# Expert stage of a hybrid trunk step: U and V rows in two rings of eight, gathers in turns, routing cut into pieces

## What is computed

```python
qh = _f32(xt @ w_q).reshape(PEER_TBLOCK, PEER_HEADS, 2, PEER_HALF)
s = jnp.einsum('thpd,hpnd->thpn', qh, _f32(subkeys))
v_top, i_top = lax.top_k(s, PEER_TOPK)
cand = (v_top[:, :, 0, :, None] + v_top[:, :, 1, None, :]).reshape(...)
sc, pos = lax.top_k(cand, PEER_TOPK)
eidx = jnp.take_along_axis(cidx, pos, axis=-1).reshape(PEER_TBLOCK, PEER_HEADS * PEER_TOPK)
gate = jax.nn.softmax(sc, axis=-1).reshape(PEER_TBLOCK, PEER_HEADS * PEER_TOPK)
act = jax.nn.gelu(_f32(jnp.einsum('td,ted->te', xt, u_tab[eidx])))
return jnp.einsum('te,ted->td', (gate * act).astype(xt.dtype), v_tab[eidx])
```

## Time and profile before

| | us |
|---|---|
| median of 3 timed runs | 5029.88 |
| lowest and highest | 5022.36 and 5049.08 |
| profiled execution, its span (first to last instruction) | 5223.8 |
| of it PE, DVE, ACT, POOL busy | 3691.8, 2919.2, 712.4, 2823.9 |
| expert stage of layer 0 in the profiled execution | 653.7 to 2680.4 |
| expert stage of layer 1 | 3225.8 to 5223.8 |

### The profile page before, as it was taken

The page is one execution under the profiler, slowest core; times in us unless marked ns, Lnnn a source line. Parts: engine busy times, 40 slices in busy tenths (PEclk is TensorE's granted clock), DMA queues, the critical chain, the costliest instruction groups (busy, mean ns, idle before and its releaser), DMA issues. The chain is left out here.

```text
span 5223.8 us, 46315 instructions
## 1 busy us (share of the span) xinstructions
PE 3691.8 (71%) x13478; PEld 1958.6 (37%) x13478; DVE 2919.2 (56%) x7010; ACT 712.4 (14%) x2058; POOL 2823.9 (54%) x2687
## 2 busy tenths in 40 slices
PE   5987857767667757667569767677667667767765
PEld 3456433333333333333224454333333333333332
DVE  1025566556566656666640356666566666666676
ACT  0011011010111101111110331111111110111111
POOL 0000067666677676777620101777777777777765
PEclk7988978878888878888789778888888888888877
DMA  7100779889999998999851002999999999999997
GB/s 269 64 9 14 257 286 368 319 330 339 346 355 357 350 360 305 349 365 350 327 196 48 21 22 100 356 352 354 340 350 348 358 342 358 354 352 344 357 351 285
DMA packets 456668, 1476.66 MB, mean 283 GB/s; under 512 B 48180, under 2 KB 93940, under 8 KB 456212
## 3 DMA queue, kind: packets, MB, share of 16 engines
q0 software_dynamic: 368640, 1342.34, 69.5%
q1 hardware_dynamic: 87828, 131.85, 7.5%
HBM read 1469.20 MB, written 4.82 MB: 282 GB/s over the span
## 5 line engine op out<-in xcount | busy, mean ns | idle before, releaser
L1400 PE MATMUL ps<-big,y 128*128 128x512 f32 x2544 | 1288.2, 670 | 971.9 <-issue 495.1
L1579 DVE SCALAR_TENSOR_TENSOR big<-big,wrk 128x1024 f32<-128x1024 f32 x960 | 1175.3, 1226 | 688.5 <-DMA big<-in_peer_u,qk 609.7
L1493 POOL DMA_INDIRECT big<-in_peer_u,qk x960 | 1071.2, 1116 | 446.1 <-issue 276.8
L1400 PEld LDWEIGHTS ps<-big,y 128*128 128x128 f32 x2544 | 544.2, 218 | 1669.2 <-issue 1329.8
L1493 POOL DMA_INDIRECT big<-in_peer_v,qk x960 | 1001.2, 1043 | 292.7 <-issue 292.7
L1400 PE MATMUL ps<-big,diag 128*128 128x512 f32 x1248 | 548.3, 592 | 0.0
L1400 PE MATMUL ps<-mod,diag 128*128 128x512 f32 x1248 | 548.3, 592 | 0.0
L1579 DVE SCALAR_TENSOR_TENSOR mod<-mod,wrk 128x1024 f32<-128x1024 f32 x320 | 391.8, 1226 | 120.0 <-DMA mod<-in_peer_u,qk 113.1
L1493 POOL DMA_INDIRECT mod<-in_peer_u,qk x320 | 378.9, 1184 | 125.0 <-issue 91.9
L293 PE MATMUL ps<-wrk 128*128 128x512 f32 x960 | 415.1, 594 | 0.0
L1493 POOL DMA_INDIRECT mod<-in_peer_v,qk x320 | 302.8, 946 | 97.7 <-issue 95.8
(11 more groups left out here) (322 smaller groups left out, 3478.2 us busy)
## 6 DMA issues: line engine op xcount, KB each, us to landing
wrk<-in_ada_w SPq DMA_DIRECT2D x12, 2048.0 KB, 8.8
big<-in_ada_w SPq DMA_DIRECT2D x24, 1024.0 KB
big<-in_peer_u,qk POOLq DMA_INDIRECT x960
big<-in_peer_v,qk POOLq DMA_INDIRECT x960
mod<-modulation_rows SPq DMA_DIRECT2D x24, 512.0 KB, 6.6
wrk<-in_mlstm_w_in SPq DMA_DIRECT2D x6, 2048.0 KB, 8.0
wrk<-in_gla_w_in SPq DMA_DIRECT2D x6, 2048.0 KB, 8.1
lnw<-in_peer_w_q SPq DMA_DIRECT2D x8, 1024.0 KB
```

What stands on the lines that cost most here:

```text
L1400: mm = pe.matmul(m.ps[:, v_bank(b) + h, :], diag[r], ring[r][:, h * HALF:(h + 1) * HALF], start=r == 0, stop=r == rows - 1)
L1493: pool.indirect_dma_start(ring[r], None, table, bass.IndirectOffsetOnAxis(ap=stage[b][:, r:r + 1], axis=0))\
L1579: dve.scalar_tensor_tensor(out=ring[r], in0=ring[r], scalar=1.0, in1=xm[t], op0=ALU.mult, op1=ALU.mult, accum_out=act_u[b][:, r:r + 1]).th ...
```

## The change

The single ring of 16 becomes two rings of eight, one for U and one for V. POOL issues V row r of group G and U row r of group G+1 in turns, each with a wait of its own for the buffer's last use eight rows before, and reads the indices where the routing writes them. DVE's routing of group G+2 is cut into 14 pieces: the first stands in gelu, the others one behind each of the first 13 dot products of G+1. The groups now go two heads at a time through the tiles (`tile(q)` is `q // 2`), so that the two groups of a pair belong to one tile: PE sums both in the same two PSUM banks, and DVE takes the sum of a pair out once, times the gate row, and adds it to the stream X, which was multiplied by ALPHA during the first group. The accumulator tiles and their clearing by POOL go. PE works on queries three groups ahead, behind V row 3, and on scores behind V row 7; a diagonal waits for its own last use. The gate and norm rows are loaded at the stage's start into buffers of their own. The last group's V rows all go to PE, and each tile is normalised in the last turn when its last pair is summed. The core of the diff:

```diff
-    RB = TOPK
+    RU = RV = 8
     TURN = 2 * NT
     TURNS = EH // 2
-    LEAD = 2
-    LAST_PE = 6
+    GROUPS = TURN * TURNS
+    PRESET = TOPK
...
-    acc = [part(D) for _ in range(NT)]
+    gated = part(D)
+    ln_rows = part(2 * D).rearrange("p (a n) -> p a n", a=2)
     assert at[0] <= m.wrk.shape[1]
 
-    ring = [m.big[:, r * D:(r + 1) * D] for r in range(RB - 4)] + [m.mod[:, n, c, :] for n in range(2) for c in range(2)]
-    xT = [m.big[:, (RB - 4 + t) * D:(RB - 3 + t) * D].rearrange("p (k n) -> p k n", k=KD) for t in range(NT - 1)] + [m.yT[:]]
+    rows = [m.big[:, r * D:(r + 1) * D] for r in range(12)] + [m.mod[:, n, c, :] for n in range(2) for c in range(2)]
+    ring_u, ring_v = rows[0:RU], rows[RU:RU + RV]
...
-    expert = small(NT * EH * TOPK).bitcast(U32)
-    gates = m.route_gate[:]
-    stage = [small(TOPK).bitcast(U32) for _ in range(2)]
+    expert = [small(TOPK).bitcast(U32) for _ in range(TURN)]
+    gates = [m.route_gate[:, q * TOPK:(q + 1) * TOPK] for q in range(TURN)]
...
+    tile = lambda q: (q % TURN) // 2
+    sum_bank = lambda q: 6 * (tile(q) % 2)
+    pairs_at = lambda n, q: n * NT + q // 2
...
             load_heads(0)
             sp.dma_start(sk, a["subkeysT"][layer]).then_inc(sk_in, 16)
+            load_rows(sp, m, a, layer, 3, (2,), "ffn", rows_in, ln_rows)
             with sp.Fori(1, TURNS) as n:
                 load_heads(n)
 
-            sp.wait_ge(route_pe.sem, route_pe.at((EH - 1) * NT - 1, "qh"))
-            load_rows(sp, m, a, layer, 3, (2,), "ffn", rows_in)
             sp.wait_ge(rows_in, 16 * 4)
...
+            def sum_v(n, q, r):
+                G, b = n * TURN + q, sum_bank(q)
+                pair_ = pairs_at(n, q)
+                if r == 0 and q % 2 == 0:
+                    pe.wait_ge(summed, pair_ + NT - (1 if tile(q) else 0))
+                pe.wait_ge(landed_v[r % RV], (G * 2 + r // RV + 1) * 16)
+                pe.wait_ge(diagonals, G * TOPK + r + 1)
+                for h in range(2):
+                    mm = pe.matmul(m.ps[:, b + h, :], diag[r], ring_v[r % RV][:, h * HALF:(h + 1) * HALF],
+                                   start=r == 0 and q % 2 == 0, stop=r == TOPK - 1 and q % 2 == 1)
+                mm.then_inc(used_v, 1)
+
+            def group(n, q, ahead):
+                for r in range(TOPK):
+                    sum_v(n, q, r)
+                    if ahead and r == 3:
+                        queries(n, q + 3)
+                    if ahead and r == 7:
+                        scores(n, q + 3)
+
...
             def diagonal(G, b):
                 act.wait_ge(gelu.sem, gelu.at(G, "weight"))
-                act.wait_ge(used_v, G * TOPK + RB)
                 for r in range(TOPK):
+                    act.wait_ge(used_v, G * TOPK + r + 1 - TOPK + PRESET)
                     act.activation(diag[r], m.ident, ACT.Copy, scale=wv[b][:, r:r + 1]).then_inc(diagonals, 1)
 
-            def group(n, q, routed):
+            def group(n, q, scored, routed, finished):
                 G, b = n * TURN + q, q % 2
-                if routed:
-                    scores(G + LEAD, b, False)
                 tanh_(G, b)
                 diagonal(G, b)
+                if finished:
+                    layer_norm_sqrt(act, m, fin, fin_act, q // 2 - 1)
+                if scored:
+                    copy_queries(G + 3, 1 - b)
                 if routed:
-                    exp(G + LEAD)
+                    exp(G + 2)
+                if scored:
+                    copy_scores(G + 3, 1 - b, False)
...
+            def row_u(g, q, r):
+                pool.wait_ge(used_u, g * TOPK + r + 1 - RU)
+                pool.sem_inc(gather_passed, 1)
+                pool.indirect_dma_start(ring_u[r % RU], None, u,
+                                        bass.IndirectOffsetOnAxis(ap=expert[q % TURN][:, r:r + 1], axis=0)) \
+                    .then_inc(landed_u[r % RU], 16)
+
+            def row_v(g, q, r):
+                pool.wait_ge(used_v, g * TOPK + r + 1 - RV + PRESET)
+                pool.sem_inc(gather_passed, 1)
+                pool.indirect_dma_start(ring_v[r % RV], None, v,
+                                        bass.IndirectOffsetOnAxis(ap=expert[q % TURN][:, r:r + 1], axis=0)) \
+                    .then_inc(landed_v[r % RV], 16)
+
+            pool.wait_ge(route.sem, route.at(0, "expert"))
+            for r in range(TOPK):
+                if r < RU:
+                    pool.sem_inc(gather_passed, 1)
+                    pool.indirect_dma_start(ring_u[r], None, u,
+                                            bass.IndirectOffsetOnAxis(ap=expert[0][:, r:r + 1], axis=0)) \
+                        .then_inc(landed_u[r], 16)
+                else:
+                    row_u(0, 0, r)
+            pool.wait_ge(prep.sem, prep.at(NT - 1, "shifted"))
+
+            def group(n, q, more):
+                G = n * TURN + q
+                if more:
+                    pool.wait_ge(route.sem, route.at(G + 1, "expert"))
+                    pool.sem_inc(gather_passed, 1)
+                for r in range(TOPK):
+                    row_v(G, q, r)
+                    if more:
+                        row_u(G + 1, q + 1, r)
+
+            with pool.Fori(0, TURNS - 1) as n:
...
+            def dot(g, q, r):
+                dve.wait_ge(landed_u[r % RU], (g * 2 + r // RU + 1) * 16)
+                dve.scalar_tensor_tensor(out=ring_u[r % RU], in0=ring_u[r % RU], scalar=1.0, in1=xm[tile(q)], op0=ALU.mult,
+                                         op1=ALU.mult, accum_out=act_u[q % 2][:, r:r + 1]).then_inc(used_u, 1)
...
+            def add_sums(n, q):
+                pair_, t = pairs_at(n, q), tile(q)
+                b = sum_bank(q)
+                dve.wait_ge(used_v, (pair_ + 1) * 2 * TOPK + PRESET)
+                dve.wait_ge(summed, pair_ + NT)
+                dve.tensor_tensor(gated, flat(m.ps[:, b:b + 2, :]), m.mod[:, 2, min(t, 1), :], ALU.mult)\
+                    .then_inc(gate_sums.sem, 1)
+                dve.wait_ge(gate_sums.sem, gate_sums.at(pair_, "gated"))
+                dve.tensor_tensor(m.X[:, t, :], m.X[:, t, :], gated, ALU.add).then_inc(summed, 1)
...
+            def period(n, q, dots, routed, sums, ended=False):
+                G, b = n * TURN + q, q % 2
+                gelu_argument(G, b)
                 if routed:
-                    route_head(G + LEAD)
...
+                    route_piece(G + 2, q + 2, 0)
+                gelu_weight(G, q, b)
+                for r in range(TOPK):
+                    if dots:
+                        dot(G + 1, q + 1, r)
+                    if r == 2 and sums:
+                        add_sums(n, q - 2)
+                        if ended:
+                            finish(q // 2 - 1)
+                    if routed:
+                        route_piece(G + 2, q + 2, r + 1)
...
+            for k in range(14):
+                route_piece(0, 0, k)
+            for r in range(TOPK):
+                dot(0, 0, r)
+                route_piece(1, 1, r)
+                if r % 3 == 0 and r < 3 * NT:
+                    t = r // 3
+                    dve.wait_ge(prep.sem, prep.at(t, "scaled"))
+                    dve.tensor_scalar(m.X[:, t, :], m.X[:, t, :], ALPHA, None, ALU.mult).then_inc(summed, 1)
+            dve.wait_ge(rows_in, 16 * 4)
+            period(0, 0, True, True, False)
             with dve.Fori(0, TURNS - 1) as n:
+                for q in range(1, TURN + 1):
+                    period(n, q, True, True, q % 2 == 0)
+            for q in range(1, TURN):
+                period(TURNS - 1, q, q + 1 < TURN, q + 2 < TURN, q % 2 == 0, True)
+            add_sums(TURNS - 1, TURN - 1)
+            finish(NT - 1)
```

More of the change, by code:

```diff
@@ L700, with layer_norm @@
 NORM = "st0 st1 mv eps rstd centred gained"
-def layer_norm(nc, dve, m, order, act_order, i, y, out, ready, passed):
+def layer_norm(nc, dve, m, order, act_order, i, y, out, ready, passed, rows=None):
     stats, mv, rs = m.stat[:, 0:12], m.stat[:, 12:14], m.stat[:, 14:15]
     own = lambda step: dve.wait_ge(order.sem, order.at(i, step))
-    own(ready)
+    rows = m.lnw if rows is None else rows
+    if ready is not None:
+        own(ready)
     for h in range(2):
@@ L937, in _, with load_rows @@
                 row_groups(NT - 1)
-def load_rows(sp, m, a, layer, first, which, ln, sem):
+def load_rows(sp, m, a, layer, first, which, ln, sem, rows=None):
     for n in which:
@@ L1464, in _ @@
+                if scored:
+                    copy_scores(G + 3, 1 - b, False)
+            copy_xT(0)
+            copy_queries(0, 0)
+            copy_scores(0, 0, True)
+            for t in range(1, NT):
                 copy_xT(t)
-            exp(LEAD - 1)
+            for q in range(1, 3):
+                copy_queries(q, q % 2)
+                exp(q - 1)
+                copy_scores(q, q % 2, False)
             with act.Fori(0, TURNS - 1) as n:
+                for q in range(TURN):
+                    group(n, q, True, True, False)
```

(30 more changed lines are left out.)

298 lines of the change are left out of this document (121 added, 177 removed).

## The result

The changed kernel takes **4815.2 us** (median of four runs, 4797.9 to 4834.4) against 5026.7 for the kernel before in the same comparison (5022.4 to 5049.1): a ratio of 0.957, 95% interval 0.953 to 0.961. The forecast was 4,847 in a range of 4,550 to 5,170. The profiled execution has a span of 4829.5 us and took 4831.3.

What follows compares the result with a forecast made beforehand. POOL was taken as the bound. Periods 211 us less and fill and drain 21 more made 190 off the profiled span of 5223.8, so 5,034; times 0.963 that gave 4,847 us, range 4,550 to 5,170.

Steps and rivals of the forecast that it cites:

- fill and drain: Each expert stage's start and end: 58 us instead of 23, then 44.6 and 47.7 instead of 68.4 and 72.5.
- factor 0.963: Timed runs' median of 5029.88 over the profiled span, applied to the forecast span of 5,034 us.
- Waits of POOL removed: POOL's waits for a ring slot or for indices in each group: all 5.1 us gone.
- Dot products against gathers: DVE's dot products delay POOL's gathers by 0.40 us each, 6.4 us per group; bounds considered 0.27 to 1.05.
- upper bound of 0.53: Mean delay per dot product if gather starts fall evenly over it: period 48.6 us, time 5,005 us.
- POOL is the bound: Kernel before, each group: 34.4 us of gathers, 9.7 between them and 5.1 of waits make POOL's period.
- Covers: Indices ready with 5 us to spare; eight U and V slots cover DVE and PE, so POOL does not wait.
- The rival of no difference: POOL's waits return behind late indices or PE: period about 48.9 us, time about 5,030 us, chance 0.10.
- Pair sums and DVE's time hidden: DVE's work per group, with two sums of 1.2 us per pair, takes 34 us of 46, hidden.
- The slower rival: Every U gather starts inside a dot product and waits for its end: period 51.2, time 5,200 us, chance 0.23.
- The high bound of 1.99: A gather beside gapless dot products takes 1.99 us: 1.05 more per dot product, 16.8 per group.
- The transfers' rival: POOL keeps 1.24 us per gather and transfers at 410 GB/s bind: period 41.4, time 4,465 us, chance 0.15.

Runs made afterwards that it cites:

- ordinary execution of before: The kernel before, unchanged, profiled a second time: 5018.7 us, span 5016.9.
- last but one experiment: The kernel before with only its token tile copied to PSUM by ACT once per group: 4996.8 us, ratio 0.9918.
- PSUM kernel: The changed kernel with the token tile of the dot products copied to PSUM once per pair of groups: 4702.0 us, ratio 0.9335.
- the block of routing: The changed kernel with the routing in one block ahead of the dot products instead of pieces between them: 5017.7 us, ratio 0.9955.
- Half rows: The changed kernel with a sum over the U row replacing the dot product, and 2 KB fetched per gathered row instead of 4: 4588.9 us.

## Why the prediction came out right, point by point

The forecast's saving is right within a few us, and two of its terms are not; that they cancel is luck. Against the ordinary execution of before: periods 39 x (46.80 - 43.97) + 39 x (46.41 - 43.78) = 213 us less (forecast 211); fill and drain 54.5 + 45.3 + 54.3 + 51.5 = 205.6 in place of 185.2 (from its stage starts at 651.44 and 3111.71 and ends at 2566.88 and 5016.9), 20 more (forecast 21).

Seen as a span the forecast was far off: it says 5,034 us, the profiled execution has 4829.5, and the whole difference is the new period, 46.5 in place of 43.97 and 43.78 (39 x 2.53 + 39 x 2.72 = 205 us). The factor 0.963 then took 187 of it off again. No run bears it out for the new period: the 0.94 and 0.30 us of which that is built are the same in both executions of before. With the measured periods the same formula, factor included, gives 4,650. The forecast's own signs say as much: the waits are gone and DVE is idle for landing rows, as it said, but the starts of a group take 43.9 us (46 to 47 forecast), the mean gather 1.07 (1.15), and the rate is 386 GB/s (365).

- *Waits of POOL removed, 5.1 us.* That they go is right: nothing is left. Their size came from an unusually slow execution; in an ordinary one they are 3.2. Mis-sized by 1.9 us per group.
- *Dot products against gathers, 0.40 us each.* Mis-sized the other way. All gathers at 0.94 would be 2406; the excess of 324 us over 1,280 dot products is 0.25 each, the low bound I had written down (0.27). In place of 36.9 us per group the gathers take 34.1. They were to grow by 36.9 - 34.4 = 2.5 and grew by 34.1 - 33.7 = 0.4, so this error is 2.1 in the difference and nearly cancels the 1.9. What failed is the even spread of starts behind the upper bound of 0.53: as many gathers as dot products do start inside one (1,280), but 251 of them in its first half and 457 in its last 0.2 us. A gather that is held up ends 0.81 us after the dot product (the median in every run that reads the token from SBUF; the earlier trace rows has 0.81 too, and not 0.94), so those late starts cost next to nothing.
- *"POOL is the bound" of the kernel before.* This premise failed, though no term hung on it alone. Removing 264 us of gathers there gave 25 (last but one experiment): the order of U behind PE's V set the period, and POOL's full timeline was partly time it would have waited anyway. POOL is the bound in the changed kernel, where removing 281 us of gathers with the token in PSUM gave 113 (129 in the spans) before the transfers took over.
- *Covers.* The 5 us to spare for the indices were there, and were the thinnest indeed: at the shorter period of the PSUM kernel POOL waits for them, at no cost. Eight slots cover PE and DVE, four do not. The rival of no difference, which rested on these, did not come.
- *Pair sums and DVE's time hidden.* Right; undone, the pair sums cost 27 to 40 us, by gathers that dot products hold up longer.
- *Fill and drain.* 54.4 against 58, 45.3 and 51.5 against 44.6 and 47.7: the sum right.
- *The slower rival* did not come in the mean: with turns and pieces between them, dot products stand apart and U gathers average 1.05 us. The high bound of 1.99 per gather is real, and the block of routing makes it ten times as frequent (205 gathers against 20). But the lock that the rival describes, gathers of 1.4 us in the mean, appeared in no run with the turns: with the block they average 1.11 to 1.20.
- *The transfers' rival* was the next bound: it came when the holding up was taken away by other means, at 402 GB/s and 42.2 us rather than 410 and 41.4.

On what holds a gather up, the Trainium skill, "SBUF — State Buffer", section "Who interferes with whom", says that a DVE instruction with at most one SBUF input stays out of GpSimd's way outside its two-port modes. The trace agrees: 949 ns with one input, 953 with the second in PSUM, and the two pairs of rows at 3512 us, 0.94 us inside the sum that reads PSUM and 1.99 inside the addition that reads SBUF twice. The scaling of X at 696 us has one input and yet held a gather up; whether it ran in a two-port mode no run shows. The estimate that I had worked out from the same page, 11.6 us per group, is not borne out (4.1), since starts do not fall evenly over the dot products.

## What to carry to other kernels

An engine that is busy or issuing nearly all the time need not be the bound: shorten its work alone and see whether a wait takes the room. Where POOL issues many gathers beside two-input DVE work, count how many gathers start inside such an instruction; spreading those instructions out was worth 203 us here and keeping one operand in PSUM 113, beside 212 for the whole change. Profile the kernel before twice before a wait's size goes into a sum.

## What the runs showed of the hardware that was not expected

- One-input instructions differ: scaling X, 0.68 us, made a gather that began 0.21 us into it last 1.27 us (rows at 696 us), while the norm's instruction of the same shape, 0.83 us, left one at 0.94 (rows at 2128 us).
- PE's granted clock in steady stretches is 0.95 to 0.97 wherever V comes in turns with U, 0.81 with the turns undone, and 0.86 to 0.87 in the kernel before (0.83 in its first execution), even with its gathers freed (a mean over the two levels, 2.4 and 1.2 GHz). It went with the order of PE's work and not with the time: the kernel with the block of routing has 0.96 and takes as long as the kernel before.
- Half rows do not halve the share of the transfers: 210 GB/s take 0.72 of it, 402 take 1.02.
